# Attention's small matmuls gathered in mid-slab, and a norm's sum of squares moved to a quarter of its slab

## What is computed

```python
h = layernorm(x, emb_ln_g, emb_ln_b)
for l in range(2):                                  # "layer"
    proj = h @ w_in[l]                              # latents, gates, pool and conv inputs
    y = concat(mla(...) * silu(g), pool(...) * silu(g), conv(...) * silu(g))   # 8 MLA heads
    h = layernorm(ALPHA * h + y @ w_out[l] + b_out[l], ln_g[l], ln_b[l])
x = h + 0.5 * swiglu(rms_norm(h, ffn1_norm), ffn1_gate, ffn1_up, ffn1_down)
q, k, v, ... = split(rms_norm(x, mix_norm) @ w_in_2)     # per-head rms_norm of q and k
out = concat(forgetting_attention(6 heads), sliding_window(6 heads), memory_attention(4 heads))
x = x + out @ w_out_2
x = x + 0.5 * swiglu(rms_norm(x, ffn2_norm), ffn2_gate, ffn2_up, ffn2_down)
```

## Time and profile before

| | |
|---|---|
| median of 3 runs | 2583.37 us (2583.27 to 2583.72) |
| the profiled execution | 2582.42 us, its span 2580.63 us |
| PE busy | 2559.9 us, 99% of the span |
| DVE, ACT busy | 1781.2 us, 1360.2 us |
| granted clock of PE | 1.00 |

### The profile page before, as it was taken

The page is one execution under the profiler, slowest core; times in us unless marked ns, Lnnn a source line. Parts: engine busy times, 40 slices in busy tenths (PEclk is TensorE's granted clock), DMA queues, the critical chain, the costliest instruction groups (busy, mean ns, idle before and its releaser), DMA issues.

```text
span 2580.6 us, 39874 instructions
## 1 busy us (share of the span) xinstructions
PE 2559.9 (99%) x14224; PEld 2213.4 (86%) x14224; DVE 1781.2 (69%) x2712; ACT 1360.2 (53%) x2112; POOL 16.7 (1%) x20
## 2 busy tenths in 40 slices
PE   7999999999999999999999999999999999999999
PEld 6888888888888888888888887888888888888888
DVE  8787658777658766556666765678767665666655
ACT  5665565565566444444444554775544444444444
POOL 2000000000000000000000000000000000000000
PEclk9999999999999999999999999999999999999999
DMA  7554455454554555555554564444555545555454
GB/s 296 185 190 177 181 211 228 153 189 177 183 208 163 195 195 178 181 201 191 193 191 164 183 212 163 147 148 170 185 192 186 195 168 189 211 183 193 174 183 164
DMA packets 75435, 482.41 MB, mean 187 GB/s; under 512 B 8384, under 2 KB 10816, under 8 KB 30784
## 3 DMA queue, kind: packets, MB, share of 16 engines
q1 hardware_dynamic: 75328, 481.00, 52.1%
HBM read 477.82 MB, written 2.10 MB: 186 GB/s over the span
## 4 chain that ended last, share of the span: by engine, by line
PE 83%; DVE 1%; ACT 1%; issue 0%; ACTq 0%; DVEq 0%
PE acc L808 45%; PE acc L809 23%; PE acc L814 3%; PE acc L816 3%; PE acc L815 3%; PE score L808 1%; PE score L1080 1%; PE score L809 1%; PE head_ps L1103 0%; DVE low L1527 0%; PE turn_ps L1089 0%; PE head_ps L1104 0%; PE sums L1023 0%; ACT high L1159 0%; ACT L1438 0%
## 5 line engine op out<-in xcount | busy, mean ns | idle before, releaser
L808 PE MATMUL acc<-xs,high 128*128 128x512 f32 x4000 | 1400.6, 396 | 2.5 <-DVE xs L2011 2.3
L1527 DVE TENSOR_TENSOR low<-raw,high 128x1024 fp32r<-128x1024 f32 (+2 forms) x976 | 1079.8, 1124 | 453.4 <-ACT high L1159 429.7
L1159 ACT ACTIVATE high<-raw 128x1024 fp32r<-128x1024 f32 (+2 forms) x976 | 945.2, 976 | 506.3 <-PE acc L809 375.7
L809 PE MATMUL acc<-xs,low 128*128 128x256 f32 x4000 | 1111.2, 278 | 0.0
L808 PEld LDWEIGHTS acc<-xs,high 128*128 128x128 f32 x4000 | 750.3, 188 | 178.2 <-DVE xs L2011 3.2
L809 PEld LDWEIGHTS acc<-xs,low 128*128 128x128 f32 x4000 | 751.7, 188 | 0.6
L808 PE MATMUL acc<-hidden,high 128*128 128x512 f32 x1408 | 490.8, 395 | 0.1
L1198 ACT ACTIVATE lowsum<-acc 128x256 f32<-128x256 f32 x348 | 133.5, 384 | 520.7 <-PE acc L809 520.0
L809 PE MATMUL acc<-hidden,low 128*128 128x256 f32 x1408 | 391.2, 278 | 0.0
L808 PEld LDWEIGHTS acc<-hidden,high 128*128 128x128 f32 x1408 | 264.1, 188 | 62.7 <-DVE low L1527 0.4
L809 PEld LDWEIGHTS acc<-hidden,low 128*128 128x128 f32 x1408 | 264.6, 188 | 0.0
(11 more groups left out here) (374 smaller groups left out, 2017.9 us busy)
## 6 DMA issues: line engine op xcount, KB each, us to landing
raw<-w_up_dram SPq DMA_DIRECT2D x176, 1024.0 KB, 4.8
raw<-w_down_dram SPq DMA_DIRECT2D x128, 704.0 KB, 4.0
raw<-w_in_dram SPq DMA_DIRECT2D x78, 1024.0 KB, 4.8
raw<-w_out_dram SPq DMA_DIRECT2D x32, 1024.0 KB, 4.8
raw<-w_heads_dram SPq DMA_DIRECT2D x24, 1024.0 KB, 4.8
raw<-w_mixout_dram SPq DMA_DIRECT2D x16, 1024.0 KB, 4.8
raw<-w_mem_dram SPq DMA_DIRECT2D x8, 1024.0 KB, 4.8
raw<-w_nat_dram SPq DMA_DIRECT2D x8, 1024.0 KB, 4.8
```

What stands on the lines that cost most here:

```text
L808: eng.matmul(bank_, hi, moving, start=start, stop=False)
L809: return eng.matmul(bank_[:, S:2 * S], lo, moving[:, 0:S], start=False, stop=stop)
L1159: eng.activation(high[:, s % SPLIT, to:to + n * P], raw[:, s % RAW, at_:at_ + n * P], ACT.Copy).then_inc((highs_a, highs_b)[piece], 1)
L1527: eng.tensor_tensor(low[:, s % SPLIT, w], raw[:, s % RAW, at_:at_ + n * P], high[:, s % SPLIT, w].bitcast(F32), ALU.subtract).then_inc((lo ...
```

## The change

In `layer_steps` the values of a head move one slot back, from three to four behind its scores, so that they fall in the same slots as the turns and scores of other heads (for the head of slot 30 from the pool slab, 33, to slot 34; for the last from 43 to 44). On PE `turn` and `mixv` join `halfway`, in tile and natural slabs alike, so values, turn and scores of a slot are done one behind the other in mid-slab. In the mix the slots of the steps stay, only their place in the slab changes; second halves of `feature` stay at the start. `factor_sum` of `ffn1` moves from pair 8 to pair 4 of its slab. ACT, DVE and SP run the same code; for them only the slot of `mixv` in the layers and the times of PE's signals differ.

```diff
@@ layer_steps
     for h, slot in enumerate((24, 26, 28, 30, 34, 36, 38, 40)):
-        head_steps(put, layer * HEADS + h, slot, slot + 3)
+        head_steps(put, layer * HEADS + h, slot, slot + 4)
@@ PE, slot
                 halfway = [x for x in steps if r.kind in ("tile", "natural") and (
-                    x[0] in ("scores", "forget_turn", "cum", "decay") or x == ("factor_sum", "ffn1")
+                    x[0] in ("scores", "turn", "mixv", "forget_turn", "cum", "decay")
                     or x[0] == "feature" and x[2] == 0)]
+                quarter = [x for x in steps if x == ("factor_sum", "ffn1")]
                 for step in steps:
-                    if step not in halfway and (r.name, k) != ("mixout", 0):
+                    if step not in halfway + quarter and (r.name, k) != ("mixout", 0):
                         do(*step)
@@ PE, tile regions
                     for b in range(KT):
-                        if b == 8:
-                            for step in halfway:
-                                do(*step)
+                        for step in halfway if b == 8 else quarter if b == 4 else []:
+                            do(*step)
```

## The result

| | before | after |
|---|---|---|
| median of 4 runs | 2583.32 us (2582.74 to 2583.72) | 2609.09 us (2605.95 to 2612.15) |
| the profiled execution | 2582.42 us, span 2580.63 us | 2612.15 us, span 2610.4 us |
| ratio, 95% interval | | 1.0093 (1.0077 to 1.011) |

The forecast was 2590.5 us, range 2585.0 to 2594.5. The sign was right, the size was not: the loss is more than three times the 7.1 us of the sum.

What follows compares the result with a forecast made beforehand. PE, busy 99% of the span, was taken as the bound: its work and waits make the time. -0.45 - 0.2 + 4.05 + 3.0 + 0.7 = +7.1 us gave 2589.5 profiled, 2590.5 as median; range 2585.0 to 2594.5.

Steps and rivals of the forecast that it cites:

- Saving by merged groups: Mix slots 9 to 30, then both MLA layers: fewer separate float32 groups on PE, -0.45 and -0.2 us.
- Group starts: Mix, slots 12, 16, 20, 24, 28: PE comes sooner to banks and waits for DVE's stores, +4.05 us.
- Head norms: Mix, slots after 12, 16, 20, 24, 28: PE's feature waits for norms delayed by later turns, +3.0 us.
- Pool slab: Pool slab of each layer: third pool product waits for its tile's store, +0.35 us a layer, +0.7 together.
- B: Layers: fewer groups could leave them in the fast pace, up to -3.6 us, 2586.9; chance 0.11.
- C: Mix: new bank and norm waits don't come, as ACT and DVE finish in time, 2584.3 us; chance 0.12.
- signs of being wrong: Whole kernel: none of the listed new PE waits, or a pace change in stretches holding no group; no size.
- Later turns lengthen two of these chains: Slots 15 and 23: ACT's later copy delays softmax and store; PE waits 1.7 and 1.5 us.
- Later turns delay the head norms: Mix slots 12, 16, 20, 24, 28: ACT's later copy delays norms for the next slab's feature, 3.0 us.
- Cost nothing: First feed-forward: sum of squares at pair 4 instead of 8 makes no wait, costs 0.
- the pace below: 280 pairs a layer between regrouped groups may take either pace: 1.8 us a layer, +/-3.6, taken at 0.
- rival D: First feed-forward: sum of squares at pair 4 leaves it slow, +11.2 us, 2601.7; chance 0.09 with heavier queueing.

Runs made afterwards that it cites:

- e11: Kernel before with only the values moved to mid-slab, in the mix only, turns left at the start: 2583.53 us, ratio 0.9984.
- e4: Whole change, plus ACT doing second halves of `feature` ahead of the slot's other steps: 2594.9 us, ratio 1.0053.
- e2: Kernel before with turns and values moved to mid-slab in the two layers only, values one slot later: 2584.54 us, ratio 1.0003.
- e1: Kernel before with only the sum of squares moved, from pair 8 to pair 4: 2594.52 us, ratio 1.0035.
- e8: Whole change without the sum of squares' move, which stays at pair 8: 2595.84 us, ratio 1.0039.
- e13: The changed kernel unaltered, run once more on another chip: 2602.16 us, ratio 1.0033 to the kernel before there.
- e7: Kernel before with the sum of squares still at pair 8, but behind the wait for the second piece: 2584.42 us, ratio 1.0006.
- e3: Kernel before with values and turns moved to mid-slab in the mix only: 2594.64 us, ratio 1.0058.
- e12: Whole change plus one already met wait behind the sum of squares at pair 4: 2600.84 us, ratio 1.0054.

## Why the prediction was right or wrong

- **What bounds it, and the sign.** Right: PE's own order sets the time, and sooner arrivals at banks and norms became waits. e11, without the later turns, has none of the new ones.
- **Saving by merged groups (-0.45, -0.2).** No such saving is seen. Without it, and with the waits as they were listed, the mix would be 7.05, and e4 has 7.5: 4.4 in the slots of new banks, 3.0 in those of the late features, 0.1 in all others.
- **Group starts (+4.05).** Right in each place: slot 12 0.2 (0.19), slot 16 1.7 (1.7), slot 24 1.5 (1.5), slots 20 and 28 0.33 more than before (0.33).
- **Head norms (+3.0).** 2.9: from the turn to the feature, slots 17, 21, 25 and 29 lost 0.83, 0.18, 0.63 and 1.30, against 0.86, 0.2, 0.66 and 1.31.
- **Pool slab (+0.35 a layer).** 0.38 in layer 1 by the distance of the starts. Layer 0 is 0.32 longer and the attention of layer 1 0.82, against 0.25 each of the sum (0.35 less 0.1). In layer 1 about 0.45 of it is pace: the last 67 pairs ahead of `out`, behind the last scores and turns, ran fast in before and slow in after. e2 stays within the noise of its runs.
- **The rivals B and C.** Both fell: the waits came, and the layers didn't run faster. Two of the prediction's signs of being wrong appeared, a wait that is not on its list (`feat`) and a change of pace in stretches that hold no group: the 2.07 of `in_a` and the first feed-forward.
- **The failed step in the mix: the list of who waits behind the turn.** "Later turns lengthen two of these chains" followed ACT's copy forward to softmax and store, and "Later turns delay the head norms" to the feature of the next slab. Neither asked what stands behind the copy on ACT and is needed by PE in the same slab. In slots 14 and 22 this is the second half of `feature`. It cost 5.0 us, and 0 to 3.4 more through the granted clock, which no step had.
- **The failed step in the feed-forward: "Cost nothing".** The bounds of that line were "those of the pace below", and the price of rival D, +11.2, was right (measured 11.45). Its chance was not. It was argued from the fact that the stretch "runs fast today behind the same group", one execution at one place; e1 is slow in eight of ten by its times, and its profile shows this stretch slow. D should have stood beside the forecast: both paces were in the rows, and nothing bounded which one a stretch takes.
- **Together.** 2583.3 + 12.5 (e8, all of attention) is 2595.8; the pace adds 11.4 where it comes, half clocks up to 3.4 more. The profiled execution of after, 2612.15, has all of it, and 2.1 of `in_a`; its other three, 2606 to 2609, fit but were not seen; e13's ten reach from 2593.5 to 2610.2. That all four came slow may be luck: half of e13's did not.

No version here beats the kernel before beyond its interval; e2, e7 and e11 equal it. The change to try for more would be none of these: the turn must stay early, because ACT is behind it.

## What to carry to other kernels

When a step is moved later on an engine that works in order, list for each consumer engine everything that is queued behind the step that waits for it, and ask of each who needs it and where; if the answer is the very group that was moved, it is a loop, and it costs the whole round trip. Here the values, whose only reader is a copy on DVE, could be moved freely (e11), the turns not. A long stretch of equal matmuls can have more than one pace, and a single profile at a new place is not evidence for the next: run it ten times, beside the old one.

## What the runs showed of the hardware that I had not expected

- **Two steady paces** of the same pair of fp32r matmuls, 0.3467 and 0.3533 us, at granted clock 1.00, without waits, for up to 2096 pairs: 11.5 us on the first long stretch, 13.9 on the second. Single distances differ in pattern: in the slow one they repeat as 0.361, 0.349, 0.350, in the fast one as 0.347, 0.347, 0.346 or as 0.350, 0.343.
- **The granted clock halved after 2.33 or 2.36 us** without a matmul, for 3.4 us, and not always: behind ten such waits (two each in after, e3, e8, e12 and e13) it fell six times; behind the waits of 1.5 us of the same runs never. The Trainium skill ("TensorE: Matmul & The Clock Gate", section "Part 1: The HAM clock gate") says of the slow matmuls at a kernel's start that their number changes from run to run of the same kernel. These traces show such a change in mid-kernel, behind the waits: after has two slow stretches, and e13, the same kernel, one.
- **How often the kernel before takes its longer time** differs: 2 of 21 and 3 of 23 runs on chips A and B, 17 of 25 and 15 of 25 on C and D. Each chip was used in one session, so whether the chip or the session makes it is not shown.
